# A top-4-of-32 expert layer whose weights arrive as longer runs, two ring places per transfer

## What is computed

```python
h2 = rms_norm(x, norm2_g)
logits = h2 @ w_router + b_router            # 32 experts
top_val, top_idx = lax.top_k(logits, 4)      # gates = softmax(top_val)
# for each expert e, over the tokens that chose it:
gu = xb @ w_gate_up[e] + b_gate_up[e]        # (1024, 2048)
gate = minimum(gu[:, :1024], 7); up = clip(gu[:, 1024:], -7, 7)
h = (up + 1) * gate * sigmoid(1.702 * gate)
y = h @ w_down[e] + b_down[e]                # (1024, 1024)
```

## Time and profile before

| | |
|---|---|
| median of 3 runs | 1084.68 us (1083.26 to 1085.2) |
| span of the profiled execution | 1082.8 us |
| its own time beside the span | not listed apart from the three runs; the span is 1.9 us under their median |
| TensorE busy | 1018.0 us, 94% of the span |
| weights' DMA queue (q1) | 417.62 MB in 77152 packets |
| all transfers over the span | mean 387 GB/s |
| transfers of `w_gate_up` into the ring | 252 of 1024 KB, median 19.9 us from issue to landing |
| transfers of `w_down` into the ring | 126 of 1024 KB, median 24.9 us |

### The profile page before, as it was taken

How to read it: one execution, slowest core, us unless ns; L and a number is a source line. 1 busy time by engine, 2 the same in 40 slices (tenths; PEclk the granted TensorE clock), 3 DMA queues, 4 the chain that set the end, 5 groups by cost and what they waited for, 6 DMA issues and landing times.

```text
span 1082.8 us, 12011 instructions
## 1 busy us (share of the span) xinstructions
PE 1018.0 (94%) x4585; PEld 421.3 (39%) x4585; DVE 207.1 (19%) x445; ACT 129.4 (12%) x200; POOL 10.9 (1%) x31
## 2 busy tenths in 40 slices
PE   9999899999999999999999989898999989898996
PEld 7684434343434343333333333333333333333333
DVE  2234321111111111111111111111011111111013
ACT  2461200101010100010001010010001010010002
POOL 1010000000000000000000000000000000000000
PEclk9999999999999999999999999999999999999999
DMA  9965299999999999999999999999999999999993
GB/s 335 414 237 199 100 367 413 366 403 418 417 418 417 416 417 416 417 417 419 418 419 417 417 417 418 416 417 417 419 418 419 417 417 417 417 417 417 418 419 119
DMA packets 79124, 418.99 MB, mean 387 GB/s; under 512 B 7880, under 2 KB 8416, under 8 KB 46336
## 3 DMA queue, kind: packets, MB, share of 16 engines
q1 hardware_dynamic: 77152, 417.62, 94.7%
q10 hardware_dynamic: 1808, 0.55, 0.2%
q0 software_dynamic: 144, 0.52, 0.1%
HBM read 417.62 MB, written 1.05 MB: 387 GB/s over the span
## 4 chain that ended last, share of the span: by engine, by line
PE 49%; SPq 26%; DMA 18%; issue 3%; DVE 2%; ACT 2%; DVEq 0%; ACTq 0%
PE bank L918 48%; SPq L306 21%; DMA ring<-in_w_gate_up_dram 18%; SPq L270 4%; PE bank L1240 1%; ACT area L516 1%; SPq L298 0%; DVE area L816 0%; DVE area L812 0%; DVE area L809 0%; PE bank L938 0%; DVE xn L896 0%; ACT area L437 0%; ACT area L435 0%; ACT area L433 0%
## 5 line engine op out<-in xcount | busy, mean ns | idle before, releaser
L918 PE MATMUL bank<-ring,area 128*64 128x512 f32 (+1 forms) x3088 | 708.6, 599 | 37.7 <-DMA ring<-in_w_gate_up_dram 28.3
L918 PEld LDWEIGHTS bank<-ring,area 128*64 128x64 f32 (+1 forms) x3088 | 218.7, 138 | 495.1 <-issue 397.0
L806 DVE TENSOR_SCALAR area<-bank 128x512 f32<-128x512 f32 x32 | 22.1, 692 | 503.8 <-PE bank L918 503.8
L514 ACT ACTIVATE area<-area 128x512 f32<-128x512 f32 x32 | 20.2, 630 | 539.0 <-DVE area L806 539.0
L918 PEld LDWEIGHTS bank<-masks,xn 128*128 128x128 f32 x544 | 63.3, 191 | 16.7 <-issue 13.8
L918 PE MATMUL bank<-masks,xn 128*128 128x128 f32 x544 | 69.7, 281 | 0.0
L918 PE MATMUL bank<-bias,bsel 4*128 4x512 f32 x128 | 63.6, 614 | 0.0
L821 DVE COPY wide<-bank 64x512 f32<-64x512 f32 x32 | 22.2, 693 | 205.6 <-PE bank L918 205.6
L519 ACT ACTIVATE wide<-bank 64x512 f32<-64x512 f32 x32 | 18.9, 590 | 251.5 <-PE bank L918 251.5
L918 PE MATMUL bank<-area,ring 128*128 128x256 f32 x192 | 42.0, 380 | 0.3 <-DVE area L597 0.3
L918 PEld LDWEIGHTS bank<-area,ring 128*128 128x128 f32 x192 | 36.3, 190 | 5.4 <-DVE area L597 0.6
(11 more groups left out here) (135 smaller groups left out, 285.3 us busy)
## 6 DMA issues: line engine op xcount, KB each, us to landing
ring<-in_w_gate_up_dram SPq DMA_DIRECT2D x252, 1024.0 KB, 19.9
ring<-in_w_down_dram SPq DMA_DIRECT2D x126, 1024.0 KB, 24.9
ring<-in_w_in_dram SPq DMA_DIRECT2D x8, 512.0 KB, 10.0
ring<-in_w_in_dram SPq DMA_DIRECT2D x4, 1024.0 KB, 17.0
ring<-in_w_out_dram SPq DMA_DIRECT2D x4, 1024.0 KB, 16.5
area<-in_w_gate_up_dram SPq DMA_DIRECT2D x4, 1024.0 KB, 6.8
area<-in_w_down_dram SPq DMA_DIRECT2D x2, 1024.0 KB, 8.1
xres<-in_x_dram SPq DMA_DIRECT2D x2, 512.0 KB, 3.8
```

The lines of the kernel that those rows point to most:

```text
L514: a.activation(sig, gatec, ACT.Sigmoid, scale=ALPHA).then_inc(sig_ok, 1)
L806: v.tensor_scalar(gatec, gbank[:], LIMIT, None, ALU.min).then_inc(gc, 1)
L918: return t.matmul(o, l, r, start=start, stop=stop, skip_group_check=True)
```

## The change

The weights' rows are dealt to the partitions differently. Of 256 neighbouring rows of `w_gate_up`, partition p takes rows 2p and 2p + 1, which is one run of 16 KB; of 512 neighbouring rows of `w_down` it takes rows 4p to 4p + 3, also 16 KB. In the loop one transfer of 2 MiB fills two neighbouring places, so that an expert has six weight transfers in the place of twelve; SP waits until both places are free, and TensorE waits for the even place's semaphore for both chunks. In the first 48 chunks each place still has its own transfer, now in runs of 8 KB for up and down alike.

The contraction steps are permuted to match. Step k holds features 256 (k // 2) + 2p + k % 2 (`d_step`), so the gathers, the router's transposes and `wrouter` take every second column; step f of the down matmuls holds hidden features of stride four, so the transposes of `upc` read every fourth column. The gain of the second norm is loaded as four rows of 256 and transposed by two small instructions, beside the one for the other gains. The input projection keeps its order.

```diff
-        return FIRST_PLACES.count(slot_of(n)) + n // RING + 1
+        return FIRST_PLACES.count(slot_of(n, first) & ~1) + n // RING + 1
...
+        g2rows = part(7744, 2 * P)[0:4, :]
...
-        vecs = sb("vecs", [24, P])
+        vecs = sb("vecs", [16, P])
...
+        def d_step(src, k):
+            lo = (k // 2) * 2 * P
+            return src[:, lo + k % 2:lo + 2 * P:2]
...
+            def rows_of(e, c, n):
+
+                if c < UP_CHUNKS:
+                    src = rows["wgu"][bass.ds(e * D + (c // 2) * 2 * P, 2 * P), :]
+                    return src.rearrange("(p s) f -> p s f", s=2)[:, c % 2:c % 2 + n, :]
+                c -= UP_CHUNKS
+                src = rows["wd"][bass.ds(e * F + (c // 2) * 4 * P, 4 * P), :]
+                return src.rearrange("(p s) f -> p s f", s=4)[:, 2 * (c % 2):2 * (c % 2) + 2 * n, :]
...
+                    src = rows_of(e, c, 1)
+                    dst = place(s).rearrange("p (s f) -> p s f", s=src.shape[1])
                     sp.dma_start(dst, src).then_inc(chunk_in[s], 16)
 
+            def load_expert(e, m0):
+
+                sp.wait_ge(bias_used, e - 1)
+                bias_rows(e, m0 // PER_EXPERT)
+                for c in range(0, PER_EXPERT, 2):
+                    s = slot_of(m0 + c)
+
+                    sp.wait_ge(chunks_used, e * PER_EXPERT + (c + 1) - (RING - 1))
+                    src = rows_of(e, c, 2)
+                    dst = ring[:, s * CHUNK:(s + 2) * CHUNK].rearrange("p (s f) -> p s f", s=src.shape[1])
+                    sp.dma_start(dst, src).then_inc(chunk_in[s], 16)
...
+            act.dma_start(g2rows, norm2_g.rearrange("l (r c) -> (l r) c", c=2 * P)).then_inc(vecs_in[3], 16)
...
-            act.dma_start(wrouter[:], w_router[0].rearrange("(k p) e -> p k e", p=P)).then_inc(
+            act.dma_start(wrouter[:].rearrange("p (c s) e -> p c s e", s=2), w_router[0].rearrange(
+                "(c p s) e -> p c s e", p=P, s=2)).then_inc(
...
-            t.transpose(bank[0][:, 0:24], vecs[:], ident[0:24, 0:24]).then_inc(vec_t, 1)
+            t.transpose(bank[0][:, 0:16], vecs[:], ident[0:16, 0:16])
+            for s in range(2):
+                m = t.transpose(bank[0][:, 16 + s:24:2], g2rows[:, s::2], ident[0:4, 0:4])
+            m.then_inc(vec_t, 1)
...
-                        m = mm(dst[:, k * P:(k + 1) * P], xn[:, tt, f:f + P], pick[p][:, tt, :],
+                        m = mm(dst[:, k * P:(k + 1) * P], d_step(xn[:, tt, :], 4 * kh + k),
+                               pick[p][:, tt, :],
...
-                    pe.wait_ge(chunk_in[slot], i * between + (16 * loads_of(m, False) - between))
+                    pe.wait_ge(chunk_in[slot & ~1], i * between + (16 * loads_of(m, False) - between))
...
-                    m = t.transpose(BG[:, j * P:(j + 1) * P], upc[:, j * P:(j + 1) * P], ident[:])
+                    m = t.transpose(BG[:, j * P:(j + 1) * P], upc[:, j::4], ident[:])
```

More of the change, by code:

```diff
@@ L172, in build @@
         bank = [ctx.enter_context(nc.psum_tensor(f"bank{i}", [P, HALF], F32)) for i in range(8)]
-        G1, G2, SBG, PSC = vecT[:, 0:8], vecT[:, 8:16], vecT[:, 16:20], vecT[:, 20:24]
+        G1, SBG, PSC = vecT[:, 0:8], vecT[:, 8:12], vecT[:, 12:16]
+        G2 = vecT[:, 16:24]
+        def d_step(src, k):
+            lo = (k // 2) * 2 * P
+            return src[:, lo + k % 2:lo + 2 * P:2]
         BG, BU, BY, BM = bank[4], bank[5], bank[6], bank[7]
@@ L262, in _, with bias_rows, first_expert @@
                              ).then_inc(wout_in[c], 16)
[L264 to L269, removed]
+            def rows_of(e, c, n):
[5 more added lines that the diff above has]
+                return src.rearrange("(p s) f -> p s f", s=4)[:, 2 * (c % 2):2 * (c % 2) + 2 * n, :]
+            def bias_rows(e, r):
                 sp.dma_start(bias[:, r % 2, :], rows["bgu"][bass.ds(e * 4, 4), :]).then_inc(
                     bias_in[r % 2], 16)
+            def first_expert(e):
+                if e >= 2:
+                    sp.wait_ge(bias_used, e - 1)
+                bias_rows(e, e)
                 for c in range(PER_EXPERT):
-                    m = m0 + c
-                    s = slot_of(m, first)
                     n = e * PER_EXPERT + c
-                    if first and m < PLACES:
+                    s = slot_of(n, True)
+                    if n < PLACES:
                         if 0 <= s < 4:
@@ L294, in load_expert @@
                             sp.wait_ge(wo_ok, 3)
-                    elif first:
+                    else:
                         sp.wait_ge(chunks_used, n - (PLACES - 1))
[L297 to L305, removed]
+                    src = rows_of(e, c, 1)
+                    dst = place(s).rearrange("p (s f) -> p s f", s=src.shape[1])
+                    sp.dma_start(dst, src).then_inc(chunk_in[s], 16)
+            def load_expert(e, m0):
+                sp.wait_ge(bias_used, e - 1)
+                bias_rows(e, m0 // PER_EXPERT)
[4 more added lines that the diff above has]
+                    dst = ring[:, s * CHUNK:(s + 2) * CHUNK].rearrange("p (s f) -> p s f", s=src.shape[1])
                     sp.dma_start(dst, src).then_inc(chunk_in[s], 16)
             for r in range(BODY):
-                load_expert(r, r * PER_EXPERT, True)
+                first_expert(r)
             with sp.Fori(1, NBODY) as i:
                 for r in range(BODY):
-                    load_expert(i * BODY + r, r * PER_EXPERT, False)
+                    load_expert(i * BODY + r, r * PER_EXPERT)
             for n in range(4):
@@ L388, in _ @@
             a = nc.scalar
-            for i, (src, lo, n) in enumerate(((norm1_g, 0, 8), (norm2_g, 8, 8), (sb_norm_g, 16, 4),
-                                              (pool_scale, 20, 4))):
+            for i, (src, lo, n) in enumerate(((norm1_g, 0, 8), (sb_norm_g, 8, 4),
+                                              (pool_scale, 12, 4))):
                 v = src[0, :, :] if len(src.shape) == 3 else src.rearrange("l (r c) -> (l r) c", c=P)
                 act.dma_start(vecs[lo:lo + n, :], v).then_inc(vecs_in[i], 16)
+            act.dma_start(g2rows, norm2_g.rearrange("l (r c) -> (l r) c", c=2 * P)).then_inc(vecs_in[3], 16)
             act.wait_ge(edge_c, 3)
@@ L930, in _, with turn @@
             pe.wait_ge(consts, 8)
-            t.transpose(bank[0][:, 0:24], vecs[:], ident[0:24, 0:24]).then_inc(vec_t, 1)
-            def turn(src, tt, halves=(0, 1)):
+            t.transpose(bank[0][:, 0:16], vecs[:], ident[0:16, 0:16])
+            for s in range(2):
+                m = t.transpose(bank[0][:, 16 + s:24:2], g2rows[:, s::2], ident[0:4, 0:4])
+            m.then_inc(vec_t, 1)
+            def turn(src, tt, halves=(0, 1), stepped=True):
                 for kh in halves:
@@ L938, in turn @@
                         m = t.transpose(bank[4 + 2 * tt + kh][:, k * P:(k + 1) * P],
-                                        src[:, tt, lo:lo + P], ident[:])
+                                        d_step(src[:, tt, :], 4 * kh + k) if stepped
+                                        else src[:, tt, lo:lo + P], ident[:])
                     m.then_inc(tr, 1)
@@ L943, in _ @@
                 pe.wait_ge(xn_ok, tt + 1)
-                turn(xn, tt)
+                turn(xn, tt, stepped=False)
             pe.wait_ge(tr_c, 2)
@@ L1146, in gather @@
                 for k in range(4):
-                    f = (4 * kh + k) * P
                     for tt in range(TT):
-                        m = mm(dst[:, k * P:(k + 1) * P], xn[:, tt, f:f + P], pick[p][:, tt, :],
+                        m = mm(dst[:, k * P:(k + 1) * P], d_step(xn[:, tt, :], 4 * kh + k),
+                               pick[p][:, tt, :],
                                start=(k == 0 and tt == 0), stop=(k == 3 and tt == 1))
@@ L1298, in all_tokens @@
                             for j in range(4):
-                                m = t.transpose(BG[:, j * P:(j + 1) * P],
-                                                upc[:, j * P:(j + 1) * P], ident[:])
+                                m = t.transpose(BG[:, j * P:(j + 1) * P], upc[:, j::4], ident[:])
                             m.then_inc(n_hT, 1)
```

## The result

The changed kernel takes 1069.0 us (1068.3 to 1070.0), the one before 1084.0 in the same session: a ratio of 0.986, with an interval of 0.985 to 0.988. The forecast was 1066.2, in a range of 1055 to 1081.

The account below looks back on a forecast made before the run. Weight transfers were taken to bound the kernel from the hole at 210 us on; -22.1 + 1.7 + 1.7 + 0.2 = -18.5 us gave a span of 1064.3 and a time of 1066.2 us, range 1055 to 1081.

Parts of the forecast that it names:

- Two stages, and the transfers' line from the hole at 210 us on: TensorE sets the pace until about 513 us, then weight transfers, which run back to back from the 210 us hole.
- Term 1: Weight transfers in the loop: 16 KB runs save 0.8 us an expert over 27.7 experts, -22.1 us.
- the windows: Trace windows of one weight kind: up chunks 2.49 us, down 2.56, about 9 ns a run, 0.73 us saved an expert.
- a bound that the windows contradicted: Down chunks' runs at 18.6 ns each, saving 1.5 us an expert; as a rival 1047 us, chance 0.12.
- The 0.2 us an expert left aside: Transfers' stage: 30.2 us an expert by summed engine rates against 30.4 by line 806; difference left out of the gain.
- Term 2: Loop's first transfer: SP waits for a second place, so the hole at 210 us grows, +1.7 us.
- Term 4: Start, before the first projection: two more small transposes on the path, +0.2 us.
- The hole that I had feared at expert 5: Expert 5's first transfer, issued at 242.3 us plus 2 us, against a queue busy until about 245.5: 1 us to spare.
- Term 3: Last expert: 16 TensorE instructions instead of 8 stand behind the last up landing, +1.7 us.
- The strided reads, taken at nothing: Gathers and transposes: strided loads cost nothing; rival at doubled column price 2.0 us an expert, 1107 us, chance 0.08.
- both signs that I had named: TensorE: the gather's 16 instructions still in 2.05 us and the transposes in 0.66 us.
- the 0.8 from which it would have begun to cost: TensorE's strided loads: above about 0.8 us an expert they cost beyond the forecast; above some 1.3 the kernel is slower.

Follow-up runs that it names:

- the early pair: Changed kernel with the loop's first transfer issued once its own two places are free, and the final gain's load once its place is free: 1066.9 us, ratio 0.984.
- pairing alone: Kernel before with two ring places per transfer in the loop, but its old runs and no permuted contraction: 1087.6 us, ratio 1.003.

## Why the prediction was right, point by point

**Two stages, and the transfers' line from the hole at 210 us on.** Right: expert 17 was the first late one (16 forecast), and the early pair showed that a gain at the start of the line arrives at its end.

**Term 1, the longer runs, -22.1 us.** Right in its mechanism, and in its price, 9 ns a run. The 0.8 us an expert was a little over the 0.73 that the windows gave, and 0.72 is what the last experts show. The line gained 20.3 us, so 1.8 of the 4.0 us by which the forecast of the span was too low (1064.3 against 1068.3) are here. This is the mis-sized term: I had rounded up, towards a bound that the windows contradicted.

**The 0.2 us an expert left aside.** Leaving them was right, as they are no matter of runs: all lengths show them. Unexplained they should not have stayed; they came with one transfer on four partitions.

**Term 2, +1.7 us.** Right. Chunk 33's use, which lets the first transfer go in the kernel before, came 2.2 us later for the reasons under term 4, and the rest of the 4.0 us by which that transfer was later, 1.7 to 1.8, is the second place's wait. The hole that I had feared at expert 5 didn't come: no window of 5 us from 220 to 300 us is under 403 GB/s.

**Term 3, +1.7 us.** Right: 1.8 us, with 0.1 of it the slower transposes and gathers; pairing alone showed both terms together, 3.3 of 3.4 us.

**Term 4, +0.2 us.** Right for what it priced, and the sum left out the rest: the trace has 2.2 us here. The two small transposes took 0.2 us, as forecast (from the first transpose to the sixteen it is 8.55 - 8.18 against 8.07 - 7.90). That the first one began 0.3 us later (8.18 against 7.90) I hadn't priced; here it is the load behind it, within a start that scatters by more. The other 1.7 us are one group at 83 us that took 5.40 us, where the same eight instructions take 3.70 in the kernel before and in the second trace of the changed kernel. The windows of the two traces of the changed kernel around it, columns as in the earlier trace rows, say that it is the clock and not the change:

```profile
80.00:90.00 10.00, 7.88 (x30) 3.79 (x30) 3.63 (x15) 2.64 (x6) 3.40 (x6) 0.83 0.46 193
```

```profile
80.00:90.00 10.00, 7.65 (x36) 4.15 (x35) 5.12 (x15) 3.77 (x9) 3.61 (x6) 1.00 0.48 201
```

The granted clock is 0.83 in the first and 1.00 in the second, as in the kernel before, though TensorE had been idle for 2.1 us shortly before in all three. Every trace has windows between 80 and 170 us in which part of the time is at the lower level, 1.2 GHz, and they aren't the same ones from one execution to the next with the same text: those at 80, 130 and 150 us in the first trace of the changed kernel (0.83 each), those at 120 and 150 in the second (0.66 each). Which idle time brings it about these traces don't settle. So part of what separates two single spans is this, and medians are the thing to compare. By them the forecast is 2.8 us too low, not 4.0; the profiled execution is the slowest of its four. How near the total came is in part luck: one such stretch more or fewer moves it by 1.7 us.

**The strided reads, taken at nothing.** Right for the time and wrong for the loads. I argued that two cycles a column left room; the transposes' loads are 47% dearer, and both signs that I had named failed: the gather's 16 instructions take 2.15 us and the transposes 0.75. The price of a column was misread too: in the kernel before, the transposes' loads of 128 columns took 141 ns, by the mean on its page, where the gathers' took 191, so a load's time isn't its columns alone. The rule of two hits per line of 16 bytes (the Trainium skill, *SBUF — State Buffer*, the note on cachelines under Door 1) puts the cost on the stride of four and not on the stride of two. The traces agree, with 66 ns a load for the one and 5 ns for the other. By the rows it was 0.07 us an expert, far from the 0.8 from which it would have begun to cost.

## What to carry to other kernels

When two resources both look full, find the stage in which one waits for the other, and follow that one's line back to where it last had a hole: what the line gains per item counts from there, and what starts or ends it counts once. In a stage bound by DMA, count the runs on an engine, not the transfers: here 9 ns each, from 2 to 16 KB, while transfers of 2 MiB instead of 1 gained nothing and cost a wait at either end. And look at the small transfers in the same queue, since here one of 8 KB on four partitions slowed the whole stream, and on 16 partitions it didn't.

## What the runs showed that I had not expected

8 KB of biases an expert, on four partitions, added 0.3 us to every late expert's period (29.68 us, and 29.36 without them), and on 16 partitions nearly nothing, 0.08 us (29.44). The 0.3 us are four times their own weight: as an estimate, 2 KB on each of four engines, the number by the Trainium skill's page above, at a sixteenth of 428 GB/s, are 0.08 us. Two runs show the effect and its cure; why it is that much more than the bytes, I haven't settled. Longer runs than 16 KB I didn't try.
